# NSA compression in a hybrid decoder trunk: the order of the prompt's and the cached groups

## What is computed

```python
chunks = kv_pad[:, :, :2].reshape(b, n_chunks, CMP_STRIDE, 2, NSA_KV_HEADS, NSA_HEAD_DIM)
pos_bias = jnp.einsum('rld,rlde->re', cmp_pos, w1)
pa = jnp.einsum('bnlrkd,rlde->bnrke', chunks, w1[:, :CMP_STRIDE])
pb = jnp.einsum('bnlrkd,rlde->bnrke', chunks, w1[:, CMP_STRIDE:])
hidden = jax.nn.gelu(pa[:, :-1] + pb[:, 1:] + pos_bias[:, None, :])
out = jnp.einsum('bnrke,ref->bnrkf', hidden, w2)
```

## Time and profile before

| what | value |
|---|---|
| time, median of 3 runs | 2571.89 us (2567.12 to 2574.41) |
| profiled execution | 2567.77 us, span 2566.0 us |
| TensorE busy | 94% of the span |
| VectorE, ScalarE busy | 51%, 29% |
| compression stage, layer 0 | to 308.5 us on the computing engines |
| compression stage, layer 3 | to 2135.9 us on the computing engines |

### The profile page before, as it was taken

The page is one execution under the profiler, slowest core; times in us unless marked ns, Lnnn a source line. Parts: engine busy times, 40 slices in busy tenths (PEclk is TensorE's granted clock), DMA queues, the critical chain, the costliest instruction groups (busy, mean ns, idle before and its releaser), DMA issues. The chain is left out here.

```text
span 2566.0 us, 45466 instructions
## 1 busy us (share of the span) xinstructions
PE 2415.8 (94%) x19180; PEld 2046.2 (80%) x19180; DVE 1315.0 (51%) x2346; ACT 735.4 (29%) x1773; POOL 16.4 (1%) x18
## 2 busy tenths in 40 slices
PE   8989988999999888999999898999999998989998
PEld 6568865699986756999888766899985787648998
DVE  2257384266542473665443285266541865525665
ACT  2125373211022333210232293221021445522200
POOL 0000000000000000000000011000000000000000
PEclk9989898999999978999999857999999997989999
DMA  9987616966643326566533255656672865293440
GB/s 347 310 237 162 206 52 219 353 217 227 234 164 132 99 74 251 209 235 226 177 131 132 68 148 175 249 200 244 219 214 72 178 177 157 80 313 108 171 172 29
DMA packets 287343, 472.71 MB, mean 184 GB/s; under 512 B 14956, under 2 KB 105149, under 8 KB 286662
## 3 DMA queue, kind: packets, MB, share of 16 engines
q1 hardware_dynamic: 272370, 456.04, 54.4%
q10 hardware_dynamic: 14770, 13.76, 1.7%
HBM read 448.72 MB, written 38.04 MB: 190 GB/s over the span
## 5 line engine op out<-in xcount | busy, mean ns | idle before, releaser
L631 PE MATMUL PS<-hT,ring 128*128 128x132 f32 x2048 | 249.7, 277 | 6.6 <-DVE hT L756 4.2
L631 PEld LDWEIGHTS PS<-hT,ring 128*128 128x128 f32 x2048 | 238.3, 190 | 11.9 <-issue 11.2
L631 PE MATMUL PS<-mT,arena 128*128 128x132 f32 x1536 | 184.6, 276 | 0.0
L631 PEld LDWEIGHTS PS<-mT,arena 128*128 128x128 f32 x1536 | 178.7, 190 | 0.0
L2664 PE MATMUL PS<-hT,ring 128*128 128x264 f32 x768 | 172.7, 386 | 0.1
L2664 PEld LDWEIGHTS PS<-hT,ring 128*128 128x128 f32 x768 | 145.1, 190 | 24.9 <-issue 0.4
L768 DVE TENSOR_TENSOR arena<-arena,PS 128x264 f32<-128x264 f32 x224 | 89.6, 426 | 131.1 <-PE PS L631 129.9
L715 ACT ACTIVATE arena<-arena 128x528 f32<-128x528 f32 x64 | 41.1, 642 | 312.0 <-DVE arena L768 312.0
L1479 DVE COPY arena<-PS 64x512 f32<-64x512 f32 (+1 forms) x160 | 94.2, 588 | 65.6 <-PE PS L1353 64.5
L631 PE MATMUL PS<-arena,ring 128*128 128x132 f32 x1024 | 126.9, 277 | 0.0
L631 PE MATMUL PS<-mT,ring 128*128 128x132 f32 x1024 | 125.7, 276 | 0.0
(11 more groups left out here) (485 smaller groups left out, 4368.1 us busy)
## 6 DMA issues: line engine op xcount, KB each, us to landing
arena<-in_w_ada SPq DMA_DIRECT2D x36, 2048.0 KB, 12.0
ring<-in_w_mlp_in SPq DMA_DIRECT2D x32, 2048.0 KB, 8.8
ring<-in_w_mlp_out SPq DMA_DIRECT2D x32, 2048.0 KB, 8.0
ring<-in_w_ada SPq DMA_DIRECT2D x12, 2048.0 KB, 19.5
ring<-in_ssd_w_in SPq DMA_DIRECT2D x12, 2048.0 KB, 7.9
ring<-in_nsa_w_in SPq DMA_DIRECT2D x10, 2048.0 KB, 9.8
arena<-in_cache_nsa_kv SPq DMA_DIRECT2D x64, 256.0 KB, 10.5
ring<-in_cache_nsa_kv SPq DMA_DIRECT2D x64, 256.0 KB, 7.6
```

The costliest lines, as they stand in the source:

```text
L631: ins = nc.tensor.matmul(PS[:, bank, at:at + HALF], lhs[:, k, p * 128:(p + 1) * 128], rhs[:, k, :], start=opens and k == 0, stop=closes an ...
```

## The change

`order` becomes (0,0), (0,1), (1,0), (1,1), (2,0), (2,1), (3,0), (4,0), (3,1), (4,1): the prompt's keys move from position 8 to position 7, ahead of the last cached values. A list `of_cache` says which positions are of the cache, and `cached_until(n)` counts these among the first n; the signals that only cached positions give (`pairs_moved`, `differed`, `sums_made`) are counted by it. SyncE waits for the ninth product in place of the eighth before it loads the key pages. The matmuls, copies and DMAs are the same in number and shape.

```diff
--- before.py
+++ after.py
@@ -1239,8 +1239,12 @@
             pairs = p["vc_p"]
             w1 = [x[:, 0:2048].rearrange("p (j e) -> p j e", j=16) for x in (mT_flat, hT_flat)]
             w2 = ada_tmp[:, :].rearrange("p (r f) -> p r f", r=2)
-            order = [(g, r) for g in range(5) for r in range(2)]
-            cached = 8
+            order = [(g, r) for g in range(3) for r in range(2)] + [(3, 0), (4, 0), (3, 1), (4, 1)]
+            of_cache = [g < 4 for g, r in order]
+
+            def cached_until(n):
+                return sum(of_cache[0:n])
+
             rows = lambda g: 128 if g < 4 else SEQ // CMP
             fc = [0, 256, 256, 512, 288]
 
@@ -1295,7 +1299,7 @@
                 for t in range(2):
                     src = pair[:, :, 256 * t:256 * t + 256]
                     dst = x[64 * t:64 * t + 64, j, :]
-                    if n < cached:
+                    if of_cache[n]:
                         yield dst[:, 512 * h:512 * h + 512].rearrange("p (b n) -> p b n", b=2), src
                     else:
                         dst = dst[:, 0:128].rearrange("p (b a k n) -> p b a k n", b=2, a=2, k=2)
@@ -1324,7 +1328,7 @@
                         fetched[0].on(sp.dma_start(G[0][b][0:SEQ // CMP], src[:, o:o + CMP // 2]), 16)
                     for b in range(NB):
                         stored2.on(sp.dma_start(win_s[L, b, 0:WIN - 1], a["cache_nsa_win"][L, b, 1:WIN]), 16)
-                    sp.wait_ge(mm_ready.sem, mm_ready.at(cached))
+                    sp.wait_ge(mm_ready.sem, mm_ready.at(9))
                     key_pages(sp, l, 2)
                     key_pages(sp, l, 3)
 
@@ -1396,7 +1400,7 @@
                             if n < 2:
                                 pe.wait_ge(weights_summed.sem, weights_summed.at(n + 1))
                             if n:
-                                pe.wait_ge(pairs_moved.sem, pairs_moved.at(n))
+                                pe.wait_ge(pairs_moved.sem, pairs_moved.at(cached_until(n)))
                         for u in range(2):
                             ins = nc.tensor.matmul(PS[:, 2, 0:256], w_both[:, r, j + 4 * u, :], columns(halves(j)[:, 1], u),
                                                    start=j == 0 and u == 0, stop=j == 3 and u == 1)
@@ -1420,8 +1424,8 @@
                     for n in range(len(order)):
                         for j in range(4):
 
-                            if n < cached:
-                                pe.wait_ge(differed.sem, differed.at(4 * n + j + 1))
+                            if of_cache[n]:
+                                pe.wait_ge(differed.sem, differed.at(4 * cached_until(n) + j + 1))
                                 ins = cached_product(n, j)
                             else:
                                 pe.wait_ge(pt_taken.sem, pt_taken.at(4 * n + j + 1))
@@ -1462,7 +1466,7 @@
 
                     def add_pairs(n):
 
-                        v.wait_ge(pairs_moved.sem, pairs_moved.at(n + 1))
+                        v.wait_ge(pairs_moved.sem, pairs_moved.at(cached_until(n + 1)))
                         o = PS[:, n % 2, :].rearrange("p (a n) -> p a n", a=2)
                         sums_made.on(nc.vector.tensor_tensor(o, o, bc(pairs, 1, 2), ALU.add))
 
@@ -1472,13 +1476,13 @@
                     position(0)
                     for m in range(4 * len(order)):
                         n, j = divmod(m, 4)
-                        if j == 3 and 0 < n <= cached:
+                        if j == 3 and n and of_cache[n - 1]:
                             add_pairs(n - 1)
                         v.wait_ge(pt_ready.sem, pt_ready.at(m + 1))
                         for dst, src in regroup(m, 0):
                             ins = nc.vector.tensor_copy(dst, src)
                         pt_taken.on(ins)
-                        if n < cached:
+                        if of_cache[n]:
                             differences(m)
                         if 3 <= m < 7:
                             if m == 3:
@@ -1512,13 +1516,13 @@
                                                      p["qT"][64 * h:64 * h + 64, at, y, 0:SEQ], ACT.Copy)
                         regroups(4 * n + 6, 4 * n + 7)
                         act.wait_ge(mm_ready.sem, mm_ready.at(n + 1))
-                        if n < cached:
+                        if of_cache[n]:
                             pairs_moved.on(nc.scalar.activation(pairs, PS[:, 2, 0:256], ACT.Copy))
                         regroups(4 * n + 7, 4 * n + 8)
                         if n < 2:
                             act.wait_ge(aux_taken.sem, aux_taken.at(n + 1))
-                        if n < cached:
-                            act.wait_ge(sums_made.sem, sums_made.at(n + 1))
+                        if of_cache[n]:
+                            act.wait_ge(sums_made.sem, sums_made.at(cached_until(n + 1)))
                             for e in range(2):
                                 dst = hid.rearrange("p (x q c e) -> p e x c q", x=8, q=8, e=2)[:, e]
                                 src = PS[:, n % 2, 256 * e:256 * e + 256].rearrange("p (x c q) -> p x c q", x=8, q=8)
```

## The result

The changed kernel is slower: 2584.3 us median of 20 runs against 2571.18 us of before in 20 runs beside it, ratio 1.0049 with a 95% interval of 1.0038 to 1.006. By the ratio that is 12.6 us, 10 to 15 (the medians differ by 13.1), where 16.5 were forecast.

The account below looks back on a forecast made before the run. Bound: TensorE to the last cached product, then SyncE's 32 issues. Positions 6 to 8 sum to 37.50 against 29.23, so release 8.27 us later; two layers, 16.5 us on 2571.89 gives 2588.4 us, range 2581 to 2603.

Parts of the forecast that it names:

- What bounds the stage: Compression stage, layers 0 and 3: TensorE to the last cached product, then SyncE's 32 page-load issues (19.35 us), set the end.
- Rival 2: Block's end at L1304: it waits for the compute engines, not SyncE's issues; 2570 us, no measurable change; chance 0.10.
- Rival 1: Position 7: light work loses TensorE's clock, costing 7 us more a layer, 2602 us in all; chance 0.13.
- Rival 3: Position 7: VectorE, busy 11.43 us beside heavy transposes, sets the pace; 10.9 us a layer, 2593.7 us; chance 0.05.
- The size: Both compression stages: SyncE's release comes 8.27 us later in each, 16.5 us slower in all.
- position 7, 4 x (1.03 + 0.98) + 0.78 = 8.82: Position 7: four light products (1.03) with heavy transposes (0.98), `out` of keys 0.58 and stall 0.20; 8.82 us.
- `out` of the prompt's keys: Position 8: taken as 0.58 us, no dearer than the cached keys, within a position of 14.10 us.
- the stated floor of 7.10: Bound from below of the 8.27 us: light work without stalls, 4 x (1.03 + 0.60) + 0.58 = 7.10 us a layer.
- The rigid shift: Stages behind the compression stage: all engines begin together, so they shift late by 8.27 us with nothing given back.
- The tail: Position 9 behind the release, 9.4 us at clock 0.52, ends some 10 us before SyncE; its gain falls into idle time.

Follow-up runs that it names:

- Experiments 1: Order of before; only SyncE's wait ahead of the key pages moved to the ninth product: 2591.92 us against 2569.82 of before, ratio 1.0091.
- 2: Changed order; 16 of the 32 key-page loads issued in the next (prompt) stage behind its own loads: 2563.45 us, ratio to before 0.9985.
- experiment 3: Changed order; all 32 key-page loads issued in the next (prompt) stage: 2553.43 us, ratio to before 0.995; repeated, 2555.58 us, ratio 0.9944.

## Why the prediction was right

- **What bounds the stage: right.** SyncE's last issue starts the next stage 0.40 us later in both layers of both kernels; the wait of 0.2 us at the block's line was read as it should be. Experiments 1, 2 and 3 moved the stage's end by moving nothing but SyncE's wait and issues. The issues were taken as equally long before and after; they took 0.9 us more in layer 0 and 1.0 less in layer 3, which nearly cancels.
- **Rival 2 (the block does not wait for SyncE), 0.10: out**, by the same three. Its reckoning of compute was too timid: compute ends 3.7 us earlier in layer 0, not 0.7 later, as the last tail kept its clock and position 7 was shorter.
- **Rival 1 (the clock falls in position 7), 0.13: out.** Position 7 was granted 1.00 in both layers, and so it was in all six profiles of this order, while position 8 of the old order, with light transposes in their place, lost the clock in two of six cases. By the rule of the Trainium skill ("TensorE: Matmul & The Clock Gate", part on PE-mode transpose), that transposes do not count for the clock, 2602 us would have been the forecast. The trace disagrees with it most plainly at the stage's start: by a finer reading, in stretches of 0.5 us, the clock rose between 166.0 and 166.5 us, with only transposes since 160.94. Position 7 at 1.00 fits that, but proves less, since light positions kept the clock too in four of the six cases. The rise, kernel of before:

```profile
165.50:166.00 0.50, 0.50 (x4) 0.43 (x3) 0.50 (x3) 0.33 (x1) 0.00 (x0) 0.50 1.04 246
166.00:166.50 0.50, 0.33 (x2) 0.00 (x0) 0.49 (x2) 0.13 (x1) 0.00 (x0) 0.71 1.12 286
166.50:167.00 0.50, 0.00 (x0) 0.00 (x0) 0.48 (x1) 0.49 (x2) 0.00 (x0) 1.00 1.16 246
```

- **Rival 3 (VectorE paces position 7): out.** It was busy 6.55 us of 7.6 there, and from 259 to 296 us the profile shows no wait of TensorE for another engine; as forecast, its last tiles were taken in position 8.
- **The size: 16.5 us forecast, 13.8 by the release, 12.6 by the runs.** The term that was mis-sized is position 7, 4 x (1.03 + 0.98) + 0.78 = 8.82, measured 7.65. A light product takes 0.82 us when heavy transposes follow (273.68 to 274.50), and the transposes 0.89 (274.50 to 275.39). The 1.03 was read where light transposes follow. Their weight loads of 16 rows stall: behind a heavy product the row at 287.50 has 0.33 us of idle time before it, and the heavy transposes of these positions, as at 274.50, have none. So I put the difference to the neighbour and not to the product, though no run varied it alone. Four steps at 0.29 less are 1.2 us of the 1.38 a layer. The remaining 0.23 is the `out` of the prompt's keys, 0.34 (288.10 to 288.44) and not 0.58. Even the stated floor of 7.10 was a little high: it was built with the same 1.03.
- **The rigid shift: right in layer 0** (next stage 93.0 against 92.8 us), not seen in layer 3, 3.7 us longer in the profiled run. The kernel of experiment 3 showed both lengths in its two layers, so I take it for the clock's scatter; that the change makes the long form likelier is not excluded.
- **The tail: right in kind.** Compute ended 14.3 us ahead of SyncE, forecast some 10; the difference is mostly the clock, 1.00 in place of 0.52, which the prediction had assumed to stay low.

## What to carry to other kernels

Before work is reordered, ask which engine ends the stage, and count a queue that only issues DMAs as such an engine: 32 issues at 0.6 us behind one wait are 20 us of serial time that the busy shares of the page do not count. Where two engines end nearly together, work that shortens one of them pays only once the other's release is moved out of the way; here the new order costs 13 us with the issues behind it, and together with their move into the next stage it gains 14, while the move alone gains nothing that can be measured. The spacing of an instruction group on TensorE belongs to the pair of groups, so price a group from a place where the same kind follows it. In this stage, light work at the end ran cheaper behind a heavy position than behind another light one, since the clock held.

## What the runs showed of the hardware

In these traces a wait of SyncE of 0.2 us at the block's end went with SyncE coming last, and one of 50.7 us with ScalarE coming last; from the last engine's end to the next stage it is 0.27 us when that is ScalarE and 0.40 when it is SyncE. Issue time of 32 page loads varied between 19.35 and 20.61 us for the same work, 1.3 us of scatter in a stage that ends with it. Position 8 of the old order, light work of 7.6 us, was granted 1.00 in four of six cases and 0.72 and 0.74 in the other two; position 9 behind it was at 0.50 to 0.52 in all six. The stretch behind the stage took 92 to 98 us, and those of 98 were the ones granted 0.50 to 0.53 on average.
